# Gate and up of three FFNs as seven block products in place of eight: the two-layer hybrid backbone on one core

## The reference

```
def swiglu(h, wg, wu, wd):
    return (jax.nn.silu(h @ wg) * (h @ wu)) @ wd

def ffn_sublayer(s, m, i, g, wg, wu, wd):
    h = modulate(rmsnorm(s, g), m[3 * i], m[3 * i + 1])
    return s + 0.5 * m[3 * i + 2] * swiglu(h, wg, wu, wd)
```

## Time and profile before

| | |
|---|---|
| time of three runs | 2839.61 us median (2837.65 to 2841.66) |
| the profiled execution, time | 2838.13 us |
| its span, first to last instruction | 2836.2 us |
| busy in it | PE 2715.3, PEld 2307.2, DVE 1687.2, ACT 763.9, POOL 197.8 us |
| mean granted TensorE clock | 0.983 of full speed |

### The profile page before, as it was taken

The page is one execution under the profiler, slowest core; times in us unless marked ns, Lnnn a source line. Parts: engine busy times, 40 slices in busy tenths (PEclk is TensorE's granted clock), DMA queues, the critical chain, the costliest instruction groups (busy, mean ns, idle before and its releaser), DMA issues.

```text
span 2836.2 us, 38296 instructions
## 1 busy us (share of the span) xinstructions
PE 2715.3 (96%) x15352; PEld 2307.2 (81%) x15352; DVE 1687.2 (59%) x2403; ACT 763.9 (27%) x1131; POOL 197.8 (7%) x324
## 2 busy tenths in 40 slices
PE   6999999999987999999999999999999988899998
PEld 4888888888955878888888788888887956888887
DVE  5655655668837375656556756556348845544445
ACT  4211212133147232111121412111124155322222
POOL 2000000030003210000001200000002013100001
PEclk7999999999999999999999999999999999999999
DMA  7532333321111132333322233323122111132221
GB/s 269 177 121 89 104 104 92 97 79 60 45 47 43 45 104 90 116 106 98 109 89 89 81 98 104 104 93 128 45 70 65 60 60 39 54 116 89 89 89 45
DMA packets 180757, 255.35 MB, mean 90 GB/s; under 512 B 5311, under 2 KB 128813, under 8 KB 180653
## 3 DMA queue, kind: packets, MB, share of 16 engines
q1 hardware_dynamic: 180652, 253.90, 27.8%
HBM read 251.78 MB, written 2.10 MB: 90 GB/s over the span
## 4 chain that ended last, share of the span: by engine, by line
PE 89%; DVE 5%; ACT 2%; POOL 2%; SPq 1%; issue 1%; DMA 0%; DVEq 0%; POOLq 0%; ACTq 0%
PE ps L931 27%; PE ps L932 27%; PE ps L933 27%; PE ps L1322 1%; PE ps L1346 1%; PE ps L1267 1%; POOL sqsum L922 1%; DVE nb L2142 1%; DVE h_lo L1785 1%; PE ps L1334 1%; ACT e L1639 1%; PE ps L1072 1%; ACT w_hi L1419 1%; DVE rstd L1764 1%; POOL w_lo L834 0%
## 5 line engine op out<-in xcount | busy, mean ns | idle before, releaser
L931 PE MATMUL ps<-h_hi,w_hi 128*128 128x512 f32 (+1 forms) x3040 | 1048.9, 345 | 18.7 <-DVE h_lo L1785 17.5
L933 PE MATMUL ps<-h_hi,w_lo 128*128 128x512 f32 (+1 forms) x3040 | 1042.6, 343 | 0.0
L932 PE MATMUL ps<-h_lo,w_hi 128*128 128x512 f32 (+1 forms) x2928 | 1007.1, 344 | 0.0
L931 PEld LDWEIGHTS ps<-h_hi,w_hi 128*128 128x128 f32 x3040 | 582.2, 192 | 91.6 <-issue 19.4
L933 PEld LDWEIGHTS ps<-h_hi,w_lo 128*128 128x128 f32 x3040 | 581.6, 191 | 66.1
L932 PEld LDWEIGHTS ps<-h_lo,w_hi 128*128 128x128 f32 x2928 | 561.2, 192 | 64.7 <-issue 1.5
L1884 DVE TENSOR_TENSOR prod<-sil,ps 128x512 f32<-128x512 f32 (+1 forms) x156 | 87.9, 568 | 640.3 <-PE ps L933 633.3
L931 PE MATMUL ps<-hid_hi,w_hi 128*128 128x512 f32 (+1 forms) x1248 | 432.9, 347 | 0.0
L932 PE MATMUL ps<-hid_lo,w_hi 128*128 128x512 f32 (+1 forms) x1248 | 429.2, 344 | 0.0
L933 PE MATMUL ps<-hid_hi,w_lo 128*128 128x512 f32 (+1 forms) x1248 | 429.0, 344 | 0.0
L1419 ACT ACTIVATE w_hi<-raw 128x2048 fp32r<-128x2048 f32 x158 | 297.1, 1907 | 470.9 <-PE ps L933 470.9
(11 more groups left out here) (157 smaller groups left out, 1970.2 us busy)
## 6 DMA issues: line engine op xcount, KB each, us to landing
side_raw<-in_w_ada SPq DMA_DIRECT2D x120, 512.0 KB, 3.7
raw<-in_w_ffn_gate SPq DMA_DIRECT2D x44, 1024.0 KB, 5.3
raw<-in_w_ffn_up SPq DMA_DIRECT2D x44, 1024.0 KB, 5.3
raw<-in_w_ffn_down SPq DMA_DIRECT2D x44, 1024.0 KB, 4.9
raw<-in_w_in SPq DMA_DIRECT2D x14, 1024.0 KB, 5.3
ada_buf<-in_w_ada SPq DMA_DIRECT2D x9, 1024.0 KB, 10.5
raw<-in_w_out SPq DMA_DIRECT2D x8, 1024.0 KB, 5.1
raw<-in_w_in SPq DMA_DIRECT2D x8, 512.0 KB, 5.2
```

The costliest lines, as they stand in the source:

```text
L931: mm(out, wh, xh, start=start, stop=False)
L932: mm(out, wh, xl, start=False, stop=False)
L933: return mm(out, wl, xh, start=False, stop=stop)
```

## The change

For f = 0, 1, 2 and groups 1 to 10, gate (and then up) of a group is treated as a 2 x 2 by 2 x 2 block product: the 256 features are two halves (c), the 1024 inputs two halves, and the tokens two halves of 384 (`HN`). Strassen's algebra in Winograd's form needs seven products of blocks in place of eight. Each product is 4 blocks k x 3 matmuls of 384 columns; they are made in the order 1, 6, 5, 7, 2, 3, 4, where 2, 3 and 4 go on in the banks of 1, 5 and 7 after these were read.

- Weights: a tile is split in seven parts of 512 elements (ACT high, DVE low). Three parts are sums of quarters of the tile, and a fourth overwrites a quarter (`weight_sums`, four POOL instructions). Tiles of `down` are split in four parts, whose low parts POOL makes (`low_down`). `raw` has two buffers in place of three; `w_hi` and `w_lo` are rings of 12 parts.
- Tokens: four sums of blocks of h are made once an FFN, behind group 0: `token_sum` on DVE (8 instructions), `token_sums` on POOL (16), `token_high` on ACT (4), `token_low` on DVE (4).
- Results: DVE adds the products together (`middle`, `corner`, `right`, `lower`), ACT takes products 1 and 5 out of PSUM.
- PE's order in a group is gate, down of the group before, up. `down` has 96 matmuls of 384 columns, and `half_add` three DVE instructions for each two banks.
- `side` work is cut in runs of one to six instructions between the rest. Group 0's is one run of 16, ahead of group 1's additions. f = 0 has side work in 11 groups, f = 1 in 10, f = 2 in 9.
- Small tables: the rotary and Fourier tables are loaded in each mixing in place of once.

```diff
+FAST = (0, 1, 2)
+HN = TOK // 2
+HK = KD // 2
+PRODUCTS = (1, 6, 5, 7, 2, 3, 4)
...
+    def halved(self, w, f, g):
+        banks = {}
+        for p in PRODUCTS:
+            key = (w + "p", f, g, p)
+            self.slot(key, banks.get({2: 1, 3: 5, 4: 7}.get(p)))
...
+            def weight_sums(w, f, g, it=None):
...
+                ptt(s1, a21, a22, ALU.add).then_inc(sums_made, 1)
+                pool.wait_ge(sums_made, sums(1))
+                ptt(s2, s1, a11, ALU.subtract).then_inc(sums_made, 1)
+                ptt(a21, a11, a21, ALU.subtract).then_inc(sums_made, 1)
+                pool.wait_ge(sums_made, sums(2))
+                ptt(s4, a12, s2, ALU.subtract).then_inc(sums_made, 1)
...
+                def body(g, it=None):
+                    low_down(f, g - 1, it)
+                    weight_sums("G", f, g + 1, it)
+                    weight_sums("U", f, g + 1, it)
...
+                    for p in PRODUCTS:
+                        wait_split(lambda x: (w, f, x, p), g, it)
+                        if w == "G" and p == 6:
+                            pe.wait_ge(t_ready, HK * (f + 1))
+                        wait_bank(pe, lambda x: (w + "p", f, x, p), g, it)
+                        wh, wl = wk((w, f, g, p), HK)
+                        xh, xl = operands[p]
+                        for k in range(HK):
+                            last = mm3(pt((w + "p", f, g, p), HN), wh[:, k, :], wl[:, k, :], xh[:, k, :], xl[:, k, :],
...
+                def half_down(g, it=None):
+                    pe.wait_ge(d_split, lin(pool_number, lambda x: ("D", f, x, 3), g, it))
...
+                def body(g, it=None):
+                    halved("G", g, it)
+                    half_down(g - 1, it)
+                    halved("U", g, it)
...
+                def middle(w, dst, g, it=None):
+                    wait_freed(dve, lambda x: (w + "p", f, x, 1), g, it)
+                    bank_add(w, 6, half_of(dst, 1, 0), half_of(dst, 1, 0), g, it)
+                def corner(w, dst, g, it=None):
+                    wait_freed(dve, lambda x: (w + "p", f, x, 6), g, it)
+                    bank_add(w, 7, half_of(dst, 1, 1), half_of(dst, 1, 0), g, it)
...
+                    tt(half_of(dst, 1, 1), half_of(dst, 1, 1), half_of(dst, 0, 1), ALU.add).then_inc(corner_done, 1)
...
+                def body(g, it=None):
+                    gate_phase(g, it)
+                    half_add(g - 1, range(0, 3), it)
+                    low_part("G", 1, g + 1, it)
+                    side(g, range(4, 7), it)
+                    half_add(g - 1, range(3, 6), it)
+                    side(g, range(7, 10), it)
+                    half_add(g - 1, range(6, KD), it)
+                    up_phase(g, it)
+                if f in FAST:
+                    dve.wait_ge(h_ready, 16 * NORM_OF[f] + 16)
+                    for k in range(HK):
+                        token_sum(k)
+                    for p in (1, 6, 5, 7):
+                        low_part("G", p, 1)
+                    for c in range(2):
+                        first_prod(c)
+                        token_low(2 * c)
+                        token_low(2 * c + 1)
+                    for p in (2, 3, 4):
+                        low_part("G", p, 1)
+                    hid_low(0)
+                    side(0, range(16))
+                    gate_phase(1)
```

More of the change, by code:

```diff
@@ L241, in side, with halved_tile @@
             self.slot(("side", f, g), (self.bank + 4) % 8)
+    def halved_tile(self, w, f, g):
+        self.tile((w, f, g), split=False)
+        for p in PRODUCTS:
+            self.part((w, f, g, p), 1)
+    def halved(self, w, f, g):
[3 more added lines that the diff above has]
+            self.slot(key, banks.get({2: 1, 3: 5, 4: 7}.get(p)))
+            banks[p] = self.slots[key][1]
+            self.used((w, f, g, p), key)
+            if (w, p) == ("U", 3) and g in SIDE_GROUPS[f]:
+                self.slot(("side", f, g), (self.bank + 3) % 8)
@@ new lines, in fast_ffn, with down_tile, down @@
+    def fast_ffn(self, f):
+        after = (1, 3, 4)[f]
+        if f:
+            self.tile(("G", f, 0))
+        self.tile(("U", f, 0))
+        first, second = last_slots(f)
+        for key in [(w, f, 0, c, first) for w in "gu" for c in range(2)] + [(w, f, 0, c, second) for c in range(2) for w in "gu"]:
+            self.slot(key)
+            if f == 0 and key == ("u", 0, 0, 1, 1):
+                self.ada(BETWEEN)
+        for w in "GU":
+            self.used((w, f, 0), (w.lower(), f, 0, 1, second))
+        def down_tile(g):
+            self.tile(("D", f, g), split=False)
+            for m in range(TILE // CHUNK):
+                self.part(("D", f, g, m), 1, pool=True)
+                self.used(("D", f, g, m), ("d", f, g, 4 * (m % 2) + 3, 1 if g < NG - 1 else second))
+        def down(g):
+            for j in range(KD):
+                for half in range(2):
+                    self.slot(("d", f, g, j, half))
+            self.used(("D", f, g), ("d", f, g, KD - 1, 1))
+        for g in range(1, NG):
+            self.halved_tile("G", f, g)
+            down_tile(g - 1)
+            self.halved_tile("U", f, g)
+        down_tile(NG - 1)
+        for g in range(1, NG - 1):
+            self.halved("G", f, g)
+            if g == 1 and 0 in SIDE_GROUPS[f]:
+                self.slot(("side", f, 0), (self.bank + 3) % 8)
+            down(g - 1)
+            self.halved("U", f, g)
+        self.halved("G", f, NG - 1)
+        self.halved("U", f, NG - 1)
+        down(NG - 2)
+        for s in (first, second):
+            for j in range(KD):
+                self.slot(("d", f, NG - 1, j, s))
+                if s == second and j == 3:
+                    self.slot(("stat", after, seg_order(after)[0]))
+        self.used(("D", f, NG - 1), ("d", f, NG - 1, KD - 1, second))
+        self.slot(("stat", after, seg_order(after)[1]))
@@ L570, in lin @@
             step = value(key(g + 2)) - v
+            assert all(value(key(g + 2 * n)) == v + n * step for n in range(LOOPS))
             return it * step + v
@@ L1824, in ffn, with side @@
                 i = 2 * (f % 2)
[L1826 removed]
+                def side(g, ms, it=None):
                     if g not in SIDE_GROUPS[f]:
```

752 lines of the change are left out of this document (557 added, 195 removed).

## The result

The changed kernel takes 2901.73 us (median of 4 runs, 2900.83 to 2904.88), the kernel before 2840.28 us beside it: ratio 1.022, 95% interval 1.0207 to 1.0233. It is slower by 61 us, where the forecast was 2790, some 50 faster. The span of the profiled execution is 2899.5 us, against 2836.2.

A forecast was written before the change was run, and what follows sets the result against it. The prediction took PE to bound the FFNs and summed 2838.1 - 127 + 36 + 43 - 4.5 + 3 = 2788.6 us, about 2790 on the median's scale. Its range was 2742 to 2838.

The forecast's parts named there:

- PE's saving: FFN groups: 24 matmuls fewer, 4.25 us less a group, period 46.7 us, -127 us over 3 x 10 groups.
- DVE in the loop: FFN groups: DVE needs 37.7 us itself, 46 to 47 with stops by POOL, level with PE.
- The loop named as ending last: Groups 2 to 9: up tile's load, POOL's eight instructions, down, up's first five products; 47.3 us, 48.2 with DVE late.
- The term "+36": Groups 2 to 9 of three FFNs: 1.5 us over 46.7 for each of 24 groups; bounds 0 and +154.
- The first groups: Start of each FFN's block products: PE waits 4.6 us at product 6, 10 at product 4 in f = 0 and 1.
- the wait of 2.5 us: First group of f = 2, no side run: wait for the late-loaded up tile and POOL's second sum.
- +43: First groups of three FFNs: the waits plus 2 us of lost clock for each of three; bounds +14 and +60.
- The upper bound of 60: First groups: the cost in us if each stall is half as long again.
- The ends: Ends of f = 0, 1 and 2: last tile split before down is over, -4.5 us, between 0 and -6.
- Two `raw` buffers ... covered, so 0: Mixing and f = 3: load and split hidden behind about 17 us of PE a tile; otherwise some 2 us a tile.
- The "+3" for POOL's sums in f = 2: f = 2: POOL's first sums fall on DVE's making of h, +3 us, 0 to 5.
- The slower rival: FFN groups: shared SBUF access makes DVE the bound, 53.1 us a group, 2907 us in all; chance 0.14.

The follow-up runs named there:

- e3: Changed kernel with every POOL instruction in the loops over groups 2 to 9 on a quarter of its columns (result not the reference's): 2839.1 us.
- e8: Changed kernel with token sums, weight sums and down's low parts on DVE, and the second mixing tile split behind the squares: 2865.3 us.
- e1: Changed kernel without 11 of the 16 side instructions of group 0 in the first and second FFN (result not the reference's): 2875.3 us.
- e6: Changed kernel with the low parts of every down tile made on DVE in place of POOL, result the same: 2830.0 us.
- e10: Changed kernel with down's low parts, token sums and, at the ends of the first three FFNs, the next two tiles' low parts on DVE: 2807.2 us.

## Why the prediction was wrong

The forecast and the measurement are 113 us apart on the spans. By its own steps:

**PE's saving: right.** 46.7 us a group was predicted; e3 shows 46.8 with PE never waiting.

**DVE in the loop: right in kind and size.** DVE at 46 to 47 us a group was predicted; 370.8 / 8 = 46.4 was measured. 6.8 us of it are the stops of three quarters of POOL's work (e3). DVE's own work can be estimated from e8, where POOL is silent: 358.1 / 8 = 44.8 us, less 12 additional instructions at 0.6, is 37.6 us, where 37.7 was predicted, and that leaves 8.8 us of stops, where 8 to 9 were predicted. The loop named as ending last is the one seen: 5.5 us for the load (5.3), 12.7 us for POOL's eight (13). The term "+36" was (48.2 - 46.7) x 24; measured is 1186.3 us for 24 groups, 49.4 each, or +65. So it was 29 us short: 0.6 us a group in f = 0, and 1.4 to 1.6 in f = 1 and 2. What f = 1 and 2 have more is product 4 waiting 2.0 to 3.5 us for `corner`, which the sum put at nothing; in e1 it is gone from both loops.

**The first groups: the step that failed most.** "DVE needs 8 x 0.89 us, POOL 16 instructions of 384 (1.0 us each, with DVE between them some 18 us)". That priced the stops for the loop and allowed only 2 us for them here, where both engines work from SBUF without pause. Measured: 11.1 us for the eight and 26 us for POOL's sixteen (82.3 to 108.4), and product 6 waits 14.9, 12.3 and 16.5 us, 44 in all, where 3 x 4.7 = 14 was predicted. Product 4 waits 11.6 and 12.1, near the 10 predicted. In f = 2 the wait of 2.5 us was 0.6 at product 4 and 4.8 at down, and each of the three groups waits 1.1 to 2.3 us for `xT`, which had no term. The clock cost more than the 2 us given to each of three: over group 1 the granted clock is 0.81 to 0.86, and PE is busy 52.5, 52.5 and 51.0 us where a group needs 46.7, some 16 us in all against 6. In all +43 was predicted; against 46.7 us a group it was 33.4 + 32.5 + 27.6 = 93.5. The upper bound of 60 was too low also, since it scaled each wait and did not ask how busy DVE would be: 70 of 80 us, with most of its instructions from SBUF, some at twice their time.

**The ends: wrong in sign.** "The ring in parts lets that tile be split before down is over: -4.5". The places in the ring say the opposite, and I did not work them out: with 12 chunks, parts two to four of the last down tile lie on parts one to three of the one before. With the saving of group 10 the ends should have been 17 us shorter than before; they are 18.6 longer, 36 us off. "Two `raw` buffers ... covered, so 0" holds inside the mixing and in f = 3 (within 3 us either way), but not where the mixing starts: a tile can only be loaded when the last down tile is split. In f = 0 there is also a wait of 4.3 us for `side_acc` in group 10. With DVE making the low parts (e6, e10) the end of f = 0 is shorter, 73.3 and 68.6 us against 75.0, though still over the 63.9 before. The "+3" for POOL's sums in f = 2 was a little too much: that stretch grew by 1.4 us.

**The slower rival** gave 2907, near the measured time, but by a sum that did not come about: 53.1 us a group in the loop, where it is 49.4, and the same 43 for the first groups. That the time is near is chance. Its mechanism, the lock of whole instructions, is what happened, in another place.

What stays open: why some groups in the loops of f = 1 and f = 2 are longer (up to 53.0 us, the others 48.7) while in f = 0 none is. In the long ones PE mostly waits at product 4 for DVE's `corner` and not at down. In e1 they go in f = 1 and nearly go in f = 2 (one of 50.0), though f = 2 has no side work in group 0, so that work alone doesn't explain them.

## What to carry to other kernels

Before work is given to POOL because it is idle, ask what DVE does in the same microseconds: if both read two operands from SBUF, an instruction on POOL costs DVE time as well, and the same instruction on DVE may be cheaper for both (0.69 us against 1.3 to 1.7 here). Price it for every stretch in which both work, the short ones above all, since a start-up stretch without slack passes each microsecond on to PE, and loses clock besides. But moving work to DVE helps only while DVE keeps slack: with all twelve instructions there the kernel was 46 us slower than with four (e8). Where a ring is cut into parts, write down for the last tiles which place each part takes and who holds it.

## What was not expected of the hardware

The stretching is mutual: the rows of before showed DVE stopped by POOL; here POOL is stopped as well. A sum of 384 elements on POOL takes 0.98 us alone, 1.73 beside a DVE instruction of 0.9 us and 2.51 beside one of 1.76. In the group shown POOL's parts of 512 take 1.67 us on average (6.68 / 4) where an instruction of that size took 1.30 alone (at 324.96), and a part of DVE's beside them 1.78 (at 331.45) where alone it takes 0.69. The Trainium skill, page "SBUF — State Buffer", section "Who interferes with whom", says that the one that comes second is blocked for the whole instruction of the first; these rows agree, for both directions. DVE's additions with one operand in PSUM kept their 0.55 us while POOL worked (at 333.15).
